# First experts of a two-block model: two experts together in blocks of 32 rows, 96 slots each, weights in 16 KB runs

## The reference

```python
def hier_moe(h, rg_w, rg_b, re_w, re_b, e_gate, e_up, e_down):
    ...
    v, e_idx = lax.top_k(sel, TOP_K)
    w2 = jax.nn.softmax(v, axis=-1) * p_top
    ids = g_idx * EXP_PER_GROUP + e_idx
    comb = jnp.einsum('tk,tke->te', w2, jax.nn.one_hot(ids, N_EXP, dtype=jnp.float32)).astype(h.dtype)
    y = jnp.zeros_like(xt)
    for e in range(N_EXP):
        he = jax.nn.silu(xt @ e_gate[e]) * (xt @ e_up[e])
        y = y + comb[:, e:e + 1] * (he @ e_down[e])
    return y.reshape(b_, s_, d_)
```

## Time and profile before

| | |
|---|---|
| median of 3 runs | 2341.58 us (2340.86 to 2343.79) |
| the profiled execution | 2339.87 us, span 2338.6 us |
| TensorE matmul busy | 2069.2 us, 88% |
| VectorE, ScalarE busy | 618.0 us, 309.8 us |
| DMA | 593.76 MB, mean 254 GB/s |
| stage of the first experts, first gate product to last down product | 509.64 to 864.39 us |

### The profile page before, as it was taken

How to read it: one execution, slowest core, us unless ns; L and a number is a source line. 1 busy time by engine, 2 the same in 40 slices (tenths; PEclk the granted TensorE clock), 3 DMA queues, 4 the chain that set the end, 5 groups by cost and what they waited for, 6 DMA issues and landing times.

```text
span 2338.6 us, 15908 instructions
## 1 busy us (share of the span) xinstructions
PE 2069.2 (88%) x6633; PEld 861.7 (37%) x6633; DVE 618.0 (26%) x897; ACT 309.8 (13%) x467; POOL 182.3 (8%) x140
## 2 busy tenths in 40 slices
PE   7989999859999976886999949999998989898997
PEld 3434444434444433323334523333333333333332
DVE  3580001230100105798852040111111111111112
ACT  2230000011010003332320100000000000000001
POOL 0000000000000001565530000000000000000000
PEclk9999999869999996897999969998999899999898
DMA  6121222239999981110012549999999999999995
GB/s 243 38 72 36 106 74 72 78 135 322 328 343 335 318 289 68 37 54 18 0 59 108 234 156 428 428 429 427 427 428 428 428 428 429 427 428 428 428 427 217
DMA packets 103435, 593.76 MB, mean 254 GB/s; under 512 B 5312, under 2 KB 6720, under 8 KB 78144
## 3 DMA queue, kind: packets, MB, share of 16 engines
q1 hardware_dynamic: 94432, 556.02, 59.2%
q10 hardware_dynamic: 4320, 19.90, 2.1%
q0 software_dynamic: 4608, 16.78, 1.9%
HBM read 578.00 MB, written 14.68 MB: 253 GB/s over the span
## 4 chain that ended last, share of the span: by engine, by line
PE 51%; DMA 12%; DVE 10%; ACT 3%; issue 2%; POOL 0%; ACTq 0%; DVEq 0%; POOLq 0%
PE ps L227 21%; PE ps L1715 11%; PE ps L1687 8%; DMA ring<-in_w_up 7%; DMA AR<-in_w_up 5%; PE ps L1668 4%; PE ps L236 3%; PE ps L1394 2%; DVE AR L1829 1%; PE ps L251 1%; DVE AR L1222 1%; DVE AR L1246 1%; DVE AR L1248 1%; PE ps L1301 1%; DVE AR L1840 0%
## 5 line engine op out<-in xcount | busy, mean ns | idle before, releaser
L227 PE MATMUL ps<-AR,ring 128*128 128x512 f32 x1128 | 499.1, 604 | 3.5 <-DVE AR L1237 2.3
L227 PE MATMUL ps<-ring,AR 128*128 128x512 f32 x832 | 368.4, 599 | 3.1 <-ACT AR L865 1.6
L227 PEld LDWEIGHTS ps<-AR,ring 128*128 128x128 f32 x1128 | 216.9, 193 | 285.9 <-issue 277.3
L1829 DVE TENSOR_TENSOR AR<-AR,ps 128x512 f32<-128x512 f32 x128 | 82.8, 685 | 787.7 <-PE ps L1668 787.7
L1687 PE MATMUL ps<-ring,AR 128*64 128x512 f32 x1184 | 262.6, 597 | 9.9 <-DMA ring<-in_w_up 7.3
L227 PEld LDWEIGHTS ps<-ring,AR 128*128 128x128 f32 x832 | 157.1, 192 | 192.3 <-issue 192.3
L1687 PE MATMUL ps<-AR 128*64 128x512 f32 x864 | 190.8, 593 | 7.3 <-DMA AR<-in_w_up 4.7
L1715 PE MATMUL ps<-ring,AR 128*64 128x512 f32 x576 | 150.6, 684 | 7.4 <-issue 6.6
L1687 PEld LDWEIGHTS ps<-ring,AR 128*64 128x64 f32 x1184 | 89.6, 138 | 178.3 <-issue 158.1
L236 PE MATMUL ps<-con,AR 128*128 128x128 f32 x416 | 79.7, 335 | 50.4 <-DVE AR L1840 27.1
L1668 PE MATMUL ps<-AR 64*128 64x512 f32 x256 | 106.4, 676 | 18.4 <-DVE AR L1829 17.6
(11 more groups left out here) (287 smaller groups left out, 1360.2 us busy)
## 6 DMA issues: line engine op xcount, KB each, us to landing
ring<-in_w_up SPq DMA_DIRECT2D x38, 2048.0 KB, 18.6
ring<-in_w_gate SPq DMA_DIRECT2D x36, 2048.0 KB, 20.6
ring<-in_w_down SPq DMA_DIRECT2D x36, 2048.0 KB, 24.9
AR<-in_w_gate SPq DMA_DIRECT2D x28, 2048.0 KB, 22.2
AR<-in_w_down SPq DMA_DIRECT2D x28, 2048.0 KB, 25.1
AR<-in_w_up SPq DMA_DIRECT2D x26, 2048.0 KB, 20.7
ring<-in_exp_w_gate SPq DMA_DIRECT2D x16, 2048.0 KB, 10.3
ring<-in_exp_w_up SPq DMA_DIRECT2D x16, 2048.0 KB, 9.4
```

The costliest lines, as they stand in the source:

```text
L227: x = PE.matmul(ps, l, r, start=i == 0, stop=i == len(pairs) - 1)
L1829: DV.tensor_tensor(XK[:, o:o + T], XK[:, o:o + T], CO[i % 2][:, :], ALU.add).then_inc(d_co, 1)
```

## The change

Two experts, 2p and 2p + 1, are worked on together, each with 96 slots: 192 rows in six blocks of 32, blocks 0 to 2 of the even expert and 3 to 5 of the odd one. `quarters` issues for each k four products of 32 rows, one for each quarter of TensorE's columns, into the four 32-partition parts of one bank. `gate_a` and `up_a` do blocks 0 to 3; `both_b` does blocks 4 and 5 for up and for gate; down needs three banks (blocks 0 to 3 in two halves of the columns, blocks 4 and 5 in both). A pair's rows are gathered by two indirect DMAs, of 128 and 64 rows, and the results are written by three DMAs. The order on TensorE is gate_a(p+1), tr(p), up_a(p+1), rows(p+2), both_b(p+1), down(p).

The weights are read with `runs`; since a partition then has rows 8p to 8p + 7, the transposes take every eighth column of the gathered rows and every fourth of the hidden ones. The list of loads goes by pairs, and `sp_front` issues one load more. The 0/1 matrices are made for one pair at a time, eight rounds in place of four. The limit of the branch is 96. `y_rows` has 96 rows for each expert, and the router scales the row numbers by 96/128. In the path for many tokens, not taken here, the same order of loads and the new layout of the weights are followed (transposes of h first, four buffers for the hidden rows, experts in pairs).

The diff, cut to the few path; of removed lines only those of the loads are shown, since the functions before stand above:

```diff
-FEW = 128
+FEW = 96
+PAIR = 2 * FEW
...
-        for e in range(17):
-            if e < 16:
-                load(f"eg{e}", kcols(A["exp_w_gate"][e], 0, 512), fj_g, e + 1)
-                load(f"eu{e}", kcols(A["exp_w_up"][e], 0, 512), fj_u, e + 1)
-            if e:
-                load(f"ed{e - 1}", krows(A["exp_w_down"][e - 1], 0, 4), fj_d, e)
+        for p in range(9):
+            if p < 8:
+                for e in (2 * p, 2 * p + 1):
+                    load(f"eg{e}", runs(A["exp_w_gate"][e], 0, 8), fj_g, e + 1)
+                for e in (2 * p, 2 * p + 1):
+                    load(f"eu{e}", runs(A["exp_w_up"][e], 0, 8), fj_u, e + 1)
+            if p:
+                for e in (2 * p - 2, 2 * p - 1):
+                    load(f"ed{e}", runs(A["exp_w_down"][e], 0, 4), fj_d, e + 1)
...
-            for n in range(1, at["eg1"] + 1):
+            for n in range(1, at["eu1"] + 1):
...
-            DV.tensor_tensor(row, slk, cc("e128").unsqueeze(1).to_broadcast([P, 4, 16]), ALU.add).then_inc(s_dv, dv())
+            DV.scalar_tensor_tensor(row, cc("e128").unsqueeze(1).to_broadcast([P, 4, 16]), FEW / 128.0, slk, ALU.mult, ALU.add)\
+                .then_inc(s_dv, dv())
...
+        def quarters(b, nk, jobs):
+            for k in range(nk):
+                for c, (rows, w) in enumerate(jobs):
+                    yield k, c, PE.matmul(b[32 * c:32 * c + 32, :], rows(k), w(k), start=k == 0, stop=k == nk - 1,
+                                          tile_position=(0, 32 * c), skip_group_check=True)
...
+            for p in range(8):
+                b = pe_few_bank(("ix", p))
+                PE.wait_ge(f_pb, p + 1)
+                x = PB_[p % 2].rearrange("p a e s -> p a (e s)")
+                matmuls(b[:, 0:2], [(x[:, a, 0:P], tok2[:, 2 * a:2 * a + 2]) for a in range(4)])
+                matmuls(b[0:64, 2:4], [(x[:, a, P:PAIR], tok2[:, 2 * a:2 * a + 2]) for a in range(4)]).then_inc(f_ix, 1)
...
+            def rows(p):
+                PE.wait_ge(s_xg[p % 2], 32 * (p // 2 + 1))
                 for h in range(2):
+                    b = pe_few_bank(("xt", p, h))
+                    transposes(b, [XGA[p % 2][:, 4 * h + k::8] for k in range(4)]).then_inc(f_xt, 1)
+                b = pe_few_bank(("xt", p, 2))
+                for k in range(8):
+                    x = PE.transpose(b[:, sl(k, 64)], XGB[p % 2][0:64, k::8], ident[0:64, 0:64])
+                x.then_inc(f_xt, 1)
+            def block(p, i):
+                return lambda k: XE[p % 2][:, k, 32 * i:32 * i + 32]
...
+            def gate_a(p):
+                b = pe_few_bank(("r1", p))
+                (w0, s0, n0), (w1_, s1, n1_) = weights(f"eg{2 * p}", 8), weights(f"eg{2 * p + 1}", 8)
+                PE.wait_ge(s0, n0)
+                PE.wait_ge(s1, n1_)
+                PE.wait_ge(f_xe, 3 * p + 3)
+                for k, c, x in quarters(b, KT, [(block(p, i), by_k(w0 if i < 3 else w1_)) for i in range(4)]):
+                    pass
+                x.then_inc(fj_g, 1)
...
+            def both_b(p):
+                b = pe_few_bank(("r3", p))
+                wg, wu = weights(f"eg{2 * p + 1}", 8)[0], weights(f"eu{2 * p + 1}", 8)[0]
+                for k, c, x in quarters(b, KT, [(block(p, 4 + i % 2), by_k(wu if i < 2 else wg)) for i in range(4)]):
+                    if k == KT - 1 and c == 1:
+                        x.then_inc(fj_u, 1)
+                x.then_inc(fj_g, 1)
             rows(0)
+            gate_a(0)
+            up_a(0)
+            both_b(0)
             rows(1)
+            for p in range(8):
+                if p + 1 < 8:
+                    gate_a(p + 1)
+                b = pe_few_bank(("tr", p, 0))
+                PE.wait_ge(f_hu, 2 * p + 1)
+                transposes(b, [fHA[p % 2][:, k::4] for k in range(4)]).then_inc(f_tr, 1)
+                b = pe_few_bank(("tr", p, 1))
+                PE.wait_ge(f_hu, 2 * p + 2)
+                for k in range(4):
+                    x = PE.transpose(b[:, sl(k, 64)], fHB[p % 2][0:64, k::4], ident[0:64, 0:64])
+                x.then_inc(f_tr, 1)
+                if p + 1 < 8:
+                    up_a(p + 1)
+                if p + 2 < 8:
+                    rows(p + 2)
+                if p + 1 < 8:
+                    both_b(p + 1)
+                (w0, s0, n0), (w1_, s1, n1_) = weights(f"ed{2 * p}", 4), weights(f"ed{2 * p + 1}", 4)
+                PE.wait_ge(s0, n0)
+                PE.wait_ge(s1, n1_)
+                PE.wait_ge(f_hb, 2 * p + 2)
+                def down(i, h):
+                    w = w0 if i < 3 else w1_
+                    return (lambda k: fHT[p % 2][:, k, 32 * i:32 * i + 32]), (lambda k: w[:, k, sl(h)])
+                b = pe_few_bank(("d", p, 0))
+                for k, c, x in quarters(b, 4, [down(i, 0) for i in range(4)]):
+                    pass
+                x.then_inc(f_d0, 1)
+                b = pe_few_bank(("d", p, 1))
+                for k, c, x in quarters(b, 4, [down(i, 1) for i in range(4)]):
+                    pass
+                x.then_inc(fj_d, 1)
+                b = pe_few_bank(("d", p, 2))
+                for k, c, x in quarters(b, 4, [down(4 + i % 2, i // 2) for i in range(4)]):
+                    pass
+                x.then_inc(fj_d, 1)
...
+            def rows(p):
+                x = XE[p % 2]
+                for i in range(3):
+                    AC.wait_ge(f_xt, 3 * p + i + 1)
+                    if p >= 2:
+                        AC.wait_ge(fj_g, 2 * p - 2)
+                    b = bank[f_bank["xt", p, i]][:, :].rearrange("p (k s) -> p k s", k=8 if i == 2 else 4)
+                    dst = x[:, :, P:PAIR] if i == 2 else x[:, 4 * i:4 * i + 4, 0:P]
+                    AC.activation(dst, b, ACT.Copy).then_inc(f_xe, 1)
+            def gate_a(p):
+                AC.wait_ge(fj_g, 2 * p + 1)
+                if p >= 2:
+                    AC.wait_ge(f_tr, 2 * p - 2)
+                AC.activation(fHA[p % 2], bank[f_bank["r1", p]][:, :], ACT.Silu).then_inc(f_he, 1)
+            def gate_b(p):
+                AC.wait_ge(fj_g, 2 * p + 2)
+                AC.activation(fHB[p % 2][0:64, :], bank[f_bank["r3", p]][64:128, :], ACT.Silu).then_inc(f_he, 1)
...
+                AC.wait_ge(f_ye, 3 * p + 2)
+                AC.dma_start(YD[PAIR * p:PAIR * p + P, :], fYA[p % 2]).then_inc(s_yd[p % 2], 16)
+                AC.wait_ge(f_ye, 3 * p + 3)
                 for h in range(2):
+                    AC.dma_start(YD[PAIR * p + P:PAIR * p + PAIR, sl(h)], fYB[p % 2][64 * h:64 * h + 64, :])\
+                        .then_inc(s_yd[p % 2], 16)
...
+            io = cc("iota128")[:, 0:FEW].unsqueeze(1).to_broadcast([P, 2, FEW])
+            for p in range(8):
                 for a in range(4):
+                    if p >= 2:
+                        DV.wait_ge(f_ix, p - 1)
+                    x = DV.tensor_tensor(PB_[p % 2][:, a, :, :], io, slk[:, a, 2 * p:2 * p + 2].unsqueeze(2)
+                                         .to_broadcast([P, 2, FEW]), ALU.is_equal)
                     if a == 3:
                         x.then_inc(f_pb, 1)
+                b = bank[f_bank["ix", p]]
+                DV.wait_ge(f_ix, p + 1)
+                DV.tensor_reduce(IDA[:, p:p + 1].bitcast(U32), b[:, 0:2], AX.X, ALU.add).then_inc(f_idx, 1)
+                DV.tensor_reduce(IDB[0:64, p:p + 1].bitcast(U32), b[0:64, 2:4], AX.X, ALU.add).then_inc(f_idx, 1)
...
+                for i, (g, d, n) in enumerate(((XGA, IDA, P), (XGB, IDB, PAIR - P))):
+                    PO.wait_ge(f_idx, 2 * p + i + 1)
+                    if p >= 2:
+                        PO.wait_ge(f_xt, 3 * p - 3)
+                    PO.indirect_dma_start(g[p % 2][0:n, :], None, H2D,
+                                          bass.IndirectOffsetOnAxis(d[0:n, p:p + 1].bitcast(U32), 0)).then_inc(s_xg[p % 2], 16)
```

More of the change, by code:

```diff
@@ new lines, in up_a @@
+            def up_a(p):
+                b = pe_few_bank(("r2", p))
+                (w0, s0, n0), (w1_, s1, n1_) = weights(f"eu{2 * p}", 8), weights(f"eu{2 * p + 1}", 8)
+                PE.wait_ge(s0, n0)
+                PE.wait_ge(s1, n1_)
+                for k, c, x in quarters(b, KT, [(block(p, i), by_k(w0 if i < 3 else w1_)) for i in range(4)]):
+                    pass
[5 more added lines that the diff above has]
+                    if k == KT - 1 and c == 1:
+                        x.then_inc(fj_u, 1)
+                x.then_inc(fj_g, 1)
@@ new lines, in gate_a @@
+            def gate_a(p):
[6 more added lines that the diff above has]
+                AC.activation(fHB[p % 2][0:64, :], bank[f_bank["r3", p]][64:128, :], ACT.Silu).then_inc(f_he, 1)
+            rows(0)
+            gate_a(0)
+            gate_b(0)
@@ L924, in dve_few @@
+            mul(0)
+            for p in range(8):
+                if p + 1 < 8:
+                    mul(p + 1)
+                for i in range(3):
+                    DV.wait_ge(*((f_d0, p + 1), (fj_d, 2 * p + 1), (fj_d, 2 * p + 2))[i])
+                    if p >= 2:
```

(24 more changed lines are left out.)

224 lines of the change are left out of this document (85 added, 139 removed).

## The result

| | before | after |
|---|---|---|
| median | 2342.26 us (4 runs, 2340.86 to 2343.79) | 2385.47 us (4 runs, 2381.70 to 2391.38) |
| profiled execution, span | 2339.87, 2338.6 us | 2384.22, 2382.9 us |
| stage, first gate product to last down product | 354.8 us | 393.7 us (515.90 to 909.65) |

A forecast was written before the change was run, and what follows sets the result against it. TensorE, not the busy DMA engines, was taken to bound the expert stage. +18.4 us in the stage, +4.0 ahead and +2 behind summed to +24.4 on 2341.58, so 2366 us, range 2345 to 2398 us.

The forecast's parts named there:

- The work of TensorE: Expert stage, per pair: 72 passes of 0.429 us plus 3.0 us of transposes, 33.9 us against 43.8 before.
- The clock behind the stop: Down, after the 8.6 us stop: TensorE runs at 1.2 GHz for a while, losing 2.3 us, bounds 0 and 2.9.
- the second half of the cycle: From the transposes before up_a to both_b's end: 2.1 us waiting, up_a to 38.1, rows to 40.1, both_b to 47.0.
- The landing of the odd up weight: Ahead of up_a: lands at 30.6 us, taken as 31.2 with a third of the y rows' write in between.
- T: The end of both_b, the zero from which the forecast counts the times of one cycle.
- The clock behind that wait: up_a, after 2.1 us of waiting: no clock loss counted, since 1.45 us of idle had lost nothing.
- Ahead: Before the stage: +2.1 us for slot mask rounds and +1.9 for cold transposes, together +4.0, bounds 0 and +7.
- Behind: After the stage: three y rows writes beside two weight loads, +2 us, bounds 0 and +5.
- The gain comes: Rival, expert stage: the odd down weight is there in time, 33.9 us a pair, 2268 us; chance 0.06.
- No clock loss: Rival, expert stage: stop stays without its clock loss, a load takes 7.8, cycle 44.0, 2336 to 2349 us; chance 0.12.
- Quarters overlap badly: Rival, quarter products: only two at a time, +247 us less some 15, about 2598 us; chance 0.11.
- the 20 us for the pass: Upper width of the forecast for a four-quarter pass at up to 0.464 us instead of 0.429, within +10 to +59.

The follow-up runs named there:

- experiment 3: The changed kernel with the same loads, order and four buffers, but each load given the buffer that is free first: 2333.83 us, ratio 0.9965.
- experiment 8: The changed kernel, but of each y rows write of pairs 0 to 6 only 8 rows go out: 2365.39 us in one run.
- experiment 2: The changed kernel with unread full products ahead of waits (8 ahead of down, 3 of up_a, 6 of gate_a(1)): 2364.84 us, ratio 1.0098.
- experiment 6: The changed kernel with a fifth weight buffer of 16 KB a partition, loads going to the one free first: 2286.76 us, ratio 0.9765.

## Why the prediction was right in kind and short in size

**Right:** slower; that TensorE's work falls and the stage still gets longer; and the buffer of the odd gate weight as the cause. Its stops are 7.8 to 8.4 us against 8.6, SP's issue comes right behind both_b, and giving the load another buffer removes them (experiment 3).

**The work of TensorE** was counted at 33.9 us a pair; 34.8 measured, of which the transposes are 3.5 (3.0 forecast). A pass of four quarters takes 0.43 to 0.44 us (64 instructions in 7.07, 160 in 17.38 at full clock), the value taken. The Trainium skill, "TensorE: Matmul & The Clock Gate", section on packing small matmuls, reports 3.07 and 2.38 for four row tiles and three column tiles; in this stream of products the trace shows the full fourfold, and the 75 us estimated from it did not come.

**The clock behind the stop** was 2.3 us; the 40 passes take 19.6 to 20.1 us (once 18.75) against 17.38 at full clock, so 2.2 to 2.7 (once 1.4). Right.

**What failed: the second half of the cycle** ("lands at the later of ... 30.6 ... I take a third of it between, 31.2. So another 2.1 us of waiting. up_a to 38.1"). Two terms were off:
- *The landing of the odd up weight.* up_a starts 31.9 to 33.5 us behind T in the six cycles, 32.7 in the mean, not 31.2: 9 us over six cycles. The y rows' write (512 KB landed 11.8 us behind its issue) goes through the same DMA engines, and I gave it 0.6 us; experiment 8 takes most of it away and brings the start to 31.0.
- *The clock behind that wait.* I held that a short wait costs no clock, from one row (1.45 us of idle). After 3.89 us 64 quarter products took 8.77 us instead of 7.07; so or nearly so in four of the six cycles, and less in a fifth: 7.8 us. This was a term at zero whose cover was one row.

**The rest of the +20.5 us that the stage has over the forecast** (393.7 against 373.2). In the first cycle, 39.0 us against 34.6, up_a starts 2.3 us late and runs 1.7 us long. I had counted no wait for the up weights there at all, and the cause of this one isn't the y rows: three weight loads go out together behind both_b(0) (SP's issues at 538.5), then the gathers of a pair's rows (540.89 and 542.14) and the even down weight (554.89), all through the same DMA engines; which of them costs the 2.3 us was not tested. The rest is that the products and the gathered rows' transposes take 0.1 to 0.2 more a group than counted, about 2 us, and that 2 us come back because the last cycle has no rows to transpose, which I overlooked. The six cycles were 51.3, 51.2, 48.3, 51.3, 49.8 and 47.2 us, 299.0 against 282.0. The start of 22.1 (22.6) and the end of 33.75 (34.0) fit.

**Ahead:** the first gate product came 6.3 us later than before. 2.6 of them stood already ahead of the expert code, at the load of the first gate weight (381.75 against 379.04 us) and at the router's first product (489.06 against 486.49), where nothing was changed; 3.7 remain for the 4.0 forecast, with rounds of 1.95 us (1.9).

**Behind:** +2 was forecast, −0.6 measured (16.8 us from the last product to the first transposes of the tail, 17.45 before). The timeline of after:

```profile
909.70 0.37 SPq L225 DMA_DIRECT2D ring<-in_w_up_a  x1
910.43 1.19 ACTq L969 DMA_DIRECT2D y_rows<-AR  x2
918.01 0.95 POOL L1041 DMA_INDIRECT AR<-y_rows,AR  x1 [194.41 <-issue]
```

The gathers start 8.4 us behind the last product, where it was 9.7, though a weight load went out just ahead of the last two writes. That these are of 64 rows and so smaller may be why; it was not tested.

Sum of the profiled executions: 38.9 (stage) + 3.7 + 2.6 − 0.6, less 0.3 in the rest, is 44.3 us, the difference of the spans.

**The rivals.** "The gain comes" named the right point, the load asked for before both_b ends, but not how near it was: an assignment of buffers, with no added memory, reaches part of it and a fifth buffer most. "No clock loss" is nearly experiment 2: 2365 us, where that rival had 2336 to 2349, since the odd up weight still comes late (up_a starts 31.0 to 32.4 us behind T, where that rival had 28.2). "Quarters overlap badly" fell with the 7.07 us. That the range held the time is in part luck: without the 20 us for the pass, which wasn't needed, its top would stand at +39, under the 43.2 measured. The width for one term covered what was missing in two others.

**What stays open.** Why a product behind 2.92 us of idle loses nothing and one behind 2.95 or even 1.28 us is cold was not settled; nor which transfers delay the first cycle, nor where the 2.6 us ahead of the stage come from.

## What to carry to other kernels

When an edit regroups work, redraw who frees which buffer: in a ring where load n takes the buffer of load n − 4, longer groups put the next load behind the group it is needed right after, and each such point costs a whole load, about 8 us here. Try the assignment "the buffer that is free first" before adding memory; here it was worth 52 us and the fifth buffer another 47. Price each wait with the clock that it can cost behind it, and let the writes of the same time take their share of the loads' bandwidth.

## What the runs showed of the hardware that I had not expected

- **Short waits can cost the clock.** Idle times of 2.31, 3.08 and 3.89 us were followed by 64 quarter products in 8.77 us (7.07 at full clock); behind 2.92, 2.54 and 2.18 us nothing was lost; and behind 1.50 us, in experiment 6, four passes stood about 0.85 us apart, as the rows at 624.25 and 625.03 begin to show, at a granted clock of 0.50. So the length of the idle time alone doesn't tell: 2.92 us cost nothing in the kernel after, 2.95 in experiment 3 and 1.28 in experiment 8 did, as the next two rows show. A single row in which nothing was lost proves little.

```profile
736.28 8.77 PE L824 MATMUL ps<-ring,AR 128*32 128x512 f32 x64 [2.95 <-DMA ring<-in_exp_w_up]
...
796.82 8.73 PE L812 MATMUL ps<-ring,AR 128*32 128x512 f32 x64 [1.28 <-DMA ring<-in_exp_w_up]
```

- **A wait for a load can stand under "issue"**: seven of them, 56.1 us, in the kernel after. Only SP's queue told that the load was asked for 8 us before.
- **The DMA engines' busy share says little of their limit.** At 336 GB/s it was 0.93 in the kernel before, and at 335 it was 0.89 with 16 KB runs; at 0.93 the same engines moved 373 GB/s in experiment 6. The gain of long runs showed only where the bandwidth was the bound.
- **Four quarters of TensorE's columns overlap in full**: four quarter instructions side by side, 128 x 32 with 512 columns, take 0.43 to 0.44 us together, what one full instruction takes.
